# Value products of unit k-4 ahead of the turn of unit k-3 in TensorE's attention loop

## What is computed

```
h = rmsnorm(x) * (1 + scale1(c)) + shift1(c)
p = h @ w_in                                # queries, keys and values of three branches, gates, mLSTM, pool
for each block of 128 queries, each of 8 heads:
    o_c = softmax(q kc') vc                 # compressed keys: 31 for the prompt
    o_s = softmax(q ks') vs                 # selected blocks; for the prompt all causal blocks are selected
    o_w = softmax(q kw') vw                 # window of 512: for the prompt all causal keys
    o   = g_c * o_c + g_s * o_s + g_w * o_w
x = x + gate1(c) * (concat(o, mlstm, pool) @ w_out)
x = x + gate2(c) * ((silu(a) * b) @ w_down)   with [a, b] = causal conv3(h2 @ w_up)
```

## Time and profile before

| | us |
|---|---|
| median of 3 runs | 967.74 (967.49 to 969.24) |
| profiled execution | 962.18 |
| span of the profile | 960.4 |
| TensorE busy (modelled) | 860.5 |
| VectorE, ScalarE, GpSimd busy | 494.4, 360.0, 338.1 |
| attention loop | 356 to 459 |

### The profile page before, as it was taken

One profiled execution on the slowest core, in us unless ns is written; L12 is line 12 of the kernel. 1 busy time (PEld: TensorE's weight loads), 2 busy tenths in 40 slices (PEclk: granted clock), 3 DMA queues, 4 the chain that ended last, 5 costly groups with the idle time before them and its releaser, 6 DMA issues.

```text
span 960.4 us, 19099 instructions
## 1 busy us (share of the span) xinstructions
PE 860.5 (90%) x7555; PEld 756.8 (79%) x7555; DVE 494.4 (51%) x938; ACT 360.0 (37%) x684; POOL 338.1 (35%) x204
## 2 busy tenths in 40 slices
PE   4869999998998589999897999999899999998994
PEld 3658899996557465666896898888899988888993
DVE  0161456465447966776366665556321555655224
ACT  3443222224323234565324544444212444344222
POOL 0033555550000974444142233333333333333340
PEclk9579999999555557999898999999999999999997
DMA  9632787864017744442072132333232323222212
GB/s 355 260 113 86 249 263 256 265 218 141 7 43 249 284 147 89 117 114 87 23 278 67 54 102 94 105 111 93 85 101 96 102 97 110 79 76 88 89 61 90
DMA packets 72440, 128.29 MB, mean 134 GB/s; under 512 B 13653, under 2 KB 48157, under 8 KB 72097
## 3 DMA queue, kind: packets, MB, share of 16 engines
q1 hardware_dynamic: 65664, 109.65, 35.0%
q10 hardware_dynamic: 6656, 17.43, 5.2%
q0 software_dynamic: 32, 0.00, 0.0%
HBM read 121.39 MB, written 9.11 MB: 136 GB/s over the span
## 4 chain that ended last, share of the span: by engine, by line
PE 50%; DVE 25%; ACT 12%; issue 4%; SPq 4%; DMA 2%; ACTq 1%; POOL 1%; DVEq 0%; POOLq 0%
PE ps L676 30%; DVE arena L1730 5%; ACT wR L1028 4%; ACT arena L1272 4%; DVE arena L1735 3%; DVE arena L1734 3%; ACT arena L1270 2%; PE ps L844 2%; PE ps L859 2%; SPq L479 2%; DVE arena L1742 2%; PE ps L659 1%; DVE sq L1321 1%; PE ps L932 1%; PE ps L733 1%
## 5 line engine op out<-in xcount | busy, mean ns | idle before, releaser
L676 PE MATMUL ps<-hR,wR 128*128 128x260 f32 x3504 | 441.0, 286 | 30.8 <-DVE arena L1730 14.2
L676 PEld LDWEIGHTS ps<-hR,wR 128*128 128x128 f32 x3504 | 429.0, 190 | 41.9 <-DVE arena L1730 20.9
L630 POOL TENSOR_TENSOR wR<-raw,wR 128x1024 fp32r<-128x1024 f32 x95 | 227.9, 2400 | 353.7 <-ACT wR L1028 352.3
L1028 ACT ACTIVATE wR<-raw 128x1024 fp32r<-128x1024 f32 x95 | 99.7, 1051 | 104.4 <-PE ps L676 100.8
L676 PE MATMUL ps<-fR,wR 128*128 128x260 f32 x1056 | 129.7, 285 | 6.9 <-DVE fR L1744 5.0
L676 PEld LDWEIGHTS ps<-fR,wR 128*128 128x128 f32 x1056 | 128.5, 190 | 8.1 <-DVE fR L1744 5.4
L1730 DVE COPY arena<-arena 128x2 f32<-128x2 f32 x44 | 48.8, 1109 | 108.6 <-ACT arena L1272 108.6
L567 POOL TENSOR_TENSOR arena<-arena,par 128x1024 f32<-128x1024 f32 x16 | 33.5, 2095 | 89.7 <-DMA arena<-cache_keys 89.7
L1339 DVE TENSOR_REDUCE arena<-arena 128x64 f32<-128x1024 f32 x16 | 19.5, 1219 | 86.1 <-POOL arena L567 86.1
L1698 DVE TENSOR_TENSOR t<-ps,mod 128x8 f32<-128x8 f32 x24 | 4.0, 167 | 109.9 <-PE ps L676 109.9
L624 POOL TENSOR_SCALAR arena<-arena,fac 128x128 f32<-128x128 f32 (+3 forms) x32 | 40.7, 1273 | 54.7 <-DVE fac L1652 54.5
(11 more groups left out here) (339 smaller groups left out, 1034.5 us busy)
## 6 DMA issues: line engine op xcount, KB each, us to landing
raw<-weights SPq DMA_DIRECT2D x95, 512.0 KB, 3.7
arena<-cache_keys SPq DMA_DIRECT2D x128, 192.0 KB, 3.3
arena<-weights SPq DMA_DIRECT2D x24, 512.0 KB, 10.3
arena<-cache_values SPq DMA_DIRECT2D x128, 64.0 KB, 1.9
arena<-weights ACTq DMA_DIRECT2D x12, 512.0 KB, 5.5
raw<-weights ACTq DMA_DIRECT2D x12, 512.0 KB, 5.2
x<-xT SPq DMA_DIRECT2D x8, 260.0 KB, 6.0
out_y<-x SPq DMA_DIRECT2D x8, 260.0 KB, 2.2
```

The lines of the kernel that those rows point to most:

```text
L630: nc.gpsimd.tensor_tensor(wR[:, i % 2, 1, :, :], raw[:, g % RAW, :, :], wR[:, i % 2, 0, :, :].bitcast(F32), ALU.subtract).then_inc(lo_read ...
L676: last = mm(ps[:, a + half, 0:TH], wR[:, i % 2, wp, k, :], src[:, hp, j, half * TH:(half + 1) * TH], start=(j == 0 and q == 0), stop=(j == ...
L1028: A(wR[:, i % 2, 0, :, :], raw[:, g % RAW, :, :], ACT.Identity).then_inc(hi_ready, 1)
```

## The change

In each step of TensorE's loop the call for the value products of unit k-4 moves ahead of the turn of unit k-3. The functions themselves, their waits and their increments stay as they are, and no other engine's list changes.

```
             for k in range(NU + 4):
                 if k < NU:
                     scores(k)
+                if k >= 4:
+                    values(k - 4)
                 if 3 <= k < NU + 3:
                     flip(k - 3)
-                if k >= 4:
-                    values(k - 4)
```

## The result

| | before | changed |
|---|---|---|
| median of plain runs, us | 967.62 (967.21 to 969.24) | 975.99 (975.06 to 980.66) |
| profiled execution, us | 962.18 | 975.97 |
| span of the profile, us | 960.4 | 974.2 |
| attention loop, first score matmul to the first matmul behind it, us | 356.08 to 459.59: 103.51 | 356.60 to 473.11: 116.51 |

The ratio is 1.0083, with a 95% interval of 1.006 to 1.0105: slower by 8.4 us. The forecast was 981.0 with a range of 974.5 to 987.

A forecast was written before the change was run, and what follows sets the result against it. TensorE was taken to bound the attention loop; 15.66 us of new waits less 2.4 of present ones gave 13.3, so 962.18 became 975.5, and the 5.6 to the plain-run median made it 981.0 us, range 974.5 to 987.

The forecast's parts named there:

- The bound: TensorE in the attention loop: next to no slack, so a new wait in its queue is paid in full.
- Cover: ScalarE's evacuation after each turn: hidden by scores alone for query blocks 0 and 1, not for 2 and 3.
- The round trip of 0.65: Value products of query blocks 2 and 3 wait 0.65 us for ScalarE's evacuation, beyond the covering scores.
- VectorE's copy: Value products on branch 0 wait for VectorE's copy of compressed weights: 0.98 us at query block 2, 0.46 at block 1.
- The sum: All loop waits: 10.17 us in three head pairs, 5.03 in the last, less 2.4 of now: net 13.3 us.
- From the profile to the runs: Profiled 962.18 plus 13.3 gives 975.5; adding the 5.6 it lay below the plain-run median gives 981.0 us.
- Passage from scores to value products: TensorE going from scores straight to value products: taken as zero, plus or minus 2.5 us.
- Rival (a): Clock falls in the loop, a stretch of 13.6 us costing 6.8 us more: 987.8 us; chance 0.10.
- The other open term of the clock: Low clock at 462 to 468 us: shifted by 13 us, may catch none or twice the work, plus or minus 2.
- (b): Faster: later turns find normalised probabilities ready; if scores also covered the evacuation, gain 6.6 us, 961.1; chance 0.03.
- (c): No difference: TensorE starts work behind the waiting value products, or weight loads hide the wait; 967.7 within 2; chance 0.05.

The follow-up runs named there:

- r4: Kernel before, with value products ahead of the turn only for units with query block 2 or 3: 975.8 us, ratio 1.0094 against the kernel before.
- r3: Kernel before, with value products ahead of the turn only for units with query block 0 or 1: 968.19 us, ratio 1.0028 against the kernel before.
- r7: Changed kernel with VectorE's copy of the turned compressed weights moved ahead of the normalisation: 974.05 us, ratio 1.0073 against the kernel before.
- r2: Kernel before, with value products ahead of the turn but of the unit one older (k-5): 967.23 us, ratio 1.0009 against the kernel before.
- r10: Kernel before, with the pool group's two products and their evacuation moved behind the scores and maxima of units 0 and 1: 965.69 us, ratio 0.9984.
- r1: The changed kernel run again, unaltered, beside the kernel before on the same chip: 979.0 against 966.5 us, ratio 1.0124.
- r8: Kernel before, with VectorE's copy of the turned compressed weights moved ahead of the normalisation: 966.23 us, ratio 1.0005.
- r9: Changed kernel with ScalarE's evacuation cut to 128 columns of each head and VectorE's copy ahead of the normalisation: 970.2 us, ratio 1.0028 against the kernel before.

## Why the prediction was right, and where it was off

**The bound.** TensorE filled the loop and every new wait was paid in full: measured, 11.6 us of loop for 11.3 of time.

**Cover.** That the evacuation is covered for blocks 0 and 1 and not for 2 and 3 held: V of (1,1) followed its scores without a hole (403.95 and 405.01 in the chain), and r4 carries nine tenths of the cost of a head pair (in the means of the plain runs 9.4 of 11.3 us).

**The round trip of 0.65.** Measured 0.55 in the nine that have scores as cover: from the scores at 411.67 to the value products at 412.64 is 0.97 for a group that takes 0.42. The term is 0.10 too large because I took the restart after the evacuation from the turn in the tail (0.15 us behind its end); value products restarted 0.05 behind it, as these lines of the changed kernel's timeline show:

```profile
411.67 0.49 PE L896 MATMUL ps<-arena 64*128 64x128 f32 x4
412.64 0.88 PE L932 MATMUL ps<-arena,vn 128*64 128x128 f32 x12 [0.48 <-ACT arena L1223]
```

```profile
411.78 0.81 ACT L1223 ACTIVATE arena<-ps 128x768 f32<-128x768 f32 x1 [2.98 <-PE ps L911]
```

The turn in r3 restarted 0.15 us behind its evacuation too. Why a turn takes 0.1 us more to restart than value products, no run here tells.

**VectorE's copy.** Forecast 0.98 and 0.46; measured 0.99 (406.55 to 407.96 for 0.42 of scores) and 0.49. r7 takes away both and gets 0.91 per head pair.

**The sum.** Per steady head pair 3.04 forecast net, 2.69 measured (the 0.35 of before gone in both). Tail, from the last samples on: 9.24 us before and 13.09 after, of which 0.81 is a turn that now comes behind the samples; the 3.0 that are left were forecast as 3.2. All in all 13.3 forecast and 11.6 measured: 1.2 of the 1.7 are the round trips, twelve with the tail's, 0.1 each; nearly all the rest is the unit (1,0) of the first head pair, which did not wait (the list has three waits for L1662, not four), since scores at the low clock covered it. The prediction named 0.3 us for that and left it out of the sum.

**From the profile to the runs.** The other step that was off is the last one: "it lies 5.6 below the median of the plain runs, and I apply the difference there". The median of three runs, 967.7, was on the high side of executions that spread from 962.4 to 972.9 with a mean of 966.6. Of the 5.0 us between 981.0 and the first comparison's 976.0, 2.0 are the size of the change (13.3 forecast, 11.3 by the means of all runs), 1.1 that base, and 1.9 the four runs of the changed kernel, whose median lay below the mean of its ten. The profiled executions misled too: that of the kernel before lay 4.4 us below its mean, that of the changed kernel 1.9 below. The profiles' difference of 13.8 and the runs' of 8.4 are both off the 11.6 by such luck, one up and one down, and that the range held both has luck in it as well.

**Passage from scores to value products.** It cost nothing: 1.06 us for scores of block 3 ahead of value products (403.95), and 1.06 ahead of a turn in the earlier trace rows; the bound of 2.5 us either way was wider than needed. The Trainium skill (TensorEngine Tiling (Array Packing), Key Properties) has a drain at each change of tiling mode, which charges both orders alike. These rows agree, and so does r2, with a head pair of 23.42 against 23.34.

**The clock.** Rival (a) didn't come: with waits of 0.4 to 1.4 us all along the loop TensorE kept the full clock from 377 to its end (granted 1.00 in both profiles). Behind the one wait of 4.5 us, in r2, the clock fell: granted from 396 to 403 was 0.60. The Trainium skill (TensorE: Matmul & The Clock Gate, Why this matters for your kernels) warns of long idle gaps between bursts, and r2's two rows agree. Behind the wait of 3.2 us in r10 the granted clock stayed at 1.00 (392 to 400), though 2.8 us of idle time stood ahead of the low stretch at the head of the loop; what makes the difference was not tried. What the Trainium skill says of transposes (TensorE: Matmul & The Clock Gate, Part 4), on which the rival leant, is not borne out in this mix. The other open term of the clock, the low stretch behind the loop, was small in the first profile (from the end of the loop to the end of the span 500.8 us before and 501.1 after) and not in the second (504.4).

**Rivals (b) and (c)** fell with the first profile: the weight loads that were put down to L1655, 4.2 us before, lost their label (0.5 us after), and no time was gained by it.

## What to carry to other kernels

In a software pipeline on an engine that has no slack, what counts in the order within a step is the work that stands between a producer's end and its consumer's start. Write down for each unit the round trip (wake-up, evacuation, restart) and the work that covers it, unit by unit: the mean of the scores here, 0.74 us, hides that half of the units had 0.42 and 0.63 against round trips of 0.97 and 1.18. An order that looks the same cost nothing here with the consumer one unit further back (r2), where the buffers allowed it. And four runs of a kernel whose executions differ by 7 us settle the direction of a difference of 8 to 12 but not its size: profiles compared part by part, or more runs, do.

## What had not been expected of the hardware

The same kernel is granted different amounts of low clock from one execution to the next, among runs on one chip too (mean 0.894 to 0.905 for the changed kernel in r1), and in places that have nothing to do with the change (96 and 697 us above); within one kernel a mean clock lower by 0.01 went with some 6 us more, by a straight line through the runs of the kernel before, from which single runs lie up to several us away. What decides it was not tried. The page loads of the samples bound the first third of the loop just behind TensorE: the 3 us that r10 gained there turned into a wait for a DMA, and the same DMA held TensorE for 1.0 us in r8, 2.0 in r9 and 4.5 in r2.
